# Eleven fixed homes for expert weights instead of nine and a one-time spare, sixteen experts written out, w1 and w3 split by contraction

## What is computed

```
for e in range(N_EXPERTS):                       # 16
    he = (silu(h @ w1[e]) * (h @ w3[e])) @ w2[e]  # w1, w3: 1024 x 512; w2: 512 x 1024
    out = out + combine[:, e:e + 1] * he          # 2 experts per token
```

## Time and profile before

| | us |
|---|---|
| median of 3 runs | 1133.92 (1132.99 to 1134.44) |
| the profiled execution | 1136.46 |
| its span, first to last instruction | 1134.6 |
| PE busy | 942.2 (83%) |
| DVE, ACT, POOL busy | 453.2, 248.2, 194.6 |
| HBM read | 306.72 MB |
| mean granted TensorE clock | 0.922 |

### The profile page before, as it was taken

How to read it: one execution, slowest core, us unless ns; L and a number is a source line. 1 busy time by engine, 2 the same in 40 slices (tenths; PEclk the granted TensorE clock), 3 DMA queues, 4 the chain that set the end, 5 groups by cost and what they waited for, 6 DMA issues and landing times.

```text
span 1134.6 us, 24010 instructions
## 1 busy us (share of the span) xinstructions
PE 942.2 (83%) x9000; PEld 550.9 (49%) x9001; DVE 453.2 (40%) x1074; ACT 248.2 (22%) x491; POOL 194.6 (17%) x328
## 2 busy tenths in 40 slices
PE   3999999988898499979888589999998477875795
PEld 2536446555445366645545266543654244442353
DVE  2178425555554423323222486416732422221223
ACT  2100112443322122313212131123521021210121
POOL 4100000110010144434323320001100111110011
PEclk9999999999989599999889789999998598997898
DMA  9997602830003989999999978317504989999991
GB/s 348 391 405 269 258 36 75 313 123 1 1 1 119 373 312 408 420 417 424 420 420 417 375 299 312 137 44 267 235 1 149 360 347 415 407 424 426 423 417 64
DMA packets 52335, 313.47 MB, mean 276 GB/s; under 512 B 6620, under 2 KB 7328, under 8 KB 33456
## 3 DMA queue, kind: packets, MB, share of 16 engines
q1 hardware_dynamic: 41168, 286.27, 62.7%
q0 software_dynamic: 8480, 18.05, 4.4%
q10 hardware_dynamic: 2624, 8.27, 2.0%
HBM read 306.72 MB, written 9.50 MB: 279 GB/s over the span
## 4 chain that ended last, share of the span: by engine, by line
PE 63%; DMA 23%; DVE 5%; issue 4%; DVEq 2%; SPq 1%; ACT 1%; POOL 0%; POOLq 0%; ACTq 0%
PE ps L1961 59%; DMA ring<-in_w 12%; DMA area<-in_w 5%; DMA HT<-in_w 3%; DMA ring<-in_w_in 2%; PE ps L2241 2%; DMA area<-h_rows,area 1%; PE ps L2070 1%; PE ps L2091 1%; DMA expert_rows<-area 1%; DVE area L1628 1%; DMA area<-expert_rows 0%; PE ps L2271 0%; PE ps L2260 0%; DVE area L1465 0%
## 5 line engine op out<-in xcount | busy, mean ns | idle before, releaser
L1961 PE MATMUL ps<-ring,area 128*32 128x256 f32 x3808 | 239.2, 399 | 48.8 <-DMA ring<-in_w 25.3
L1961 PE MATMUL ps<-area 128*32 128x256 f32 (+6 forms) x2328 | 245.6, 392 | 21.8 <-DVE area L1847 9.7
L1961 PE MATMUL ps<-ring,HT 128*128 128x512 f32 (+1 forms) x576 | 259.3, 604 | 2.1 <-ACT HT L1186 1.5
L1961 PEld LDWEIGHTS ps<-ring,area 128*32 128x32 f32 x3808 | 136.6, 115 | 140.3 <-issue 47.8
L1961 PEld LDWEIGHTS ps<-ring,HT 128*128 128x128 f32 x576 | 110.5, 197 | 128.7 <-issue 127.8
L1961 PEld LDWEIGHTS ps<-area 128*32 128x32 f32 (+3 forms) x2328 | 143.2, 144 | 57.3 <-issue 35.5
L1961 PE MATMUL ps<-HT,area 128*32 128x256 f32 x704 | 89.1, 409 | 37.4 <-DMA area<-in_w 20.8
L1875 DVE STREAM_TRANSPOSE area<-area 128x256 f32<-128x256 f32 x65 | 29.0, 446 | 199.8 <-PE ps L1961 197.0
L1961 PE MATMUL ps<-HT,ring 128*128 128x256 f32 (+1 forms) x320 | 88.1, 433 | 3.6 <-DMA ring<-in_w_in 3.4
L971 POOL DMA_INDIRECT area<-h_rows,area x68 | 70.9, 1043 | 102.8 <-DVEq L1860 42.3
L1961 PEld LDWEIGHTS ps<-HT,area 128*32 128x32 f32 x704 | 48.7, 118 | 72.5 <-issue 51.7
(11 more groups left out here) (229 smaller groups left out, 800.8 us busy)
## 6 DMA issues: line engine op xcount, KB each, us to landing
ring<-in_w SPq DMA_DIRECT2D x64, 2048.0 KB
ring<-in_w_ada SPq DMA_DIRECT2D x24, 2048.0 KB
area<-in_w SPq DMA_DIRECT2D x21, 1024.0 KB
ring<-in_w_in SPq DMA_DIRECT2D x10, 2048.0 KB
HT<-in_w SPq DMA_DIRECT2D x10, 2048.0 KB
area<-in_w SPq DMA_DIRECT2D x10, 2048.0 KB
ring<-in_w_out SPq DMA_DIRECT2D x4, 2048.0 KB
area<-expert_rows ACTq DMA_DIRECT2D x8, 512.0 KB, 7.2
```

The costliest lines, as they stand in the source:

```text
L1961: return t_.matmul(out, lhsT, rhs, start=first, stop=last_)
```

## The change

There are eleven homes in one turn through all 48 units. The spare place becomes a home like the others, and the eleventh ("late") is 12 KB per partition of new SBUF, gained by cutting the space for POOL's DMA descriptors from 16 to 4 KB per partition, and 4 KB of constants (`cst`, columns 128 to 1151: triangle, ones, rotation tables, masks) that the experts' stage doesn't read. Its first load waits for the slot choices (`oh_done`). Those constants are loaded again for layer 1, and ROWS1 moves out of `cst`. All loads and all sixteen experts are written out; waits are on constants. The first unit of an expert now holds the first half of the contraction for w1 and w3 together, the second the rest, so that TensorE waits for each at its own half. The order of the homes is HT, late, area, split, spare in layer 0 and HT, area, spare, late, split in layer 1. The blocks' arithmetic is the same.

```diff
-    w = w.reshape(DEPTH, E_N, 2, NG, KD, SLOT, 2, 2, SLOT, NCF)
-    w = w.transpose(0, 1, 6, 3, 5, 4, 7, 2, 9, 8)
+    w = w.reshape(DEPTH, E_N, 2, NG, 2, KD // 2, SLOT, NG, SLOT, NCF)
+    w = w.transpose(0, 1, 4, 3, 6, 5, 7, 2, 9, 8)
...
+        turn = [order[(len(names) + n) % RING] for n in range(RING)]
+        if l == 0:
+            turn += [HT_HOME, LATE_HOME, AREA_HOME, SPLIT_HOME, SPARE_HOME]
+        else:
+            turn += [HT_HOME, AREA_HOME, SPARE_HOME, LATE_HOME, SPLIT_HOME]
+        row, last = [], {}
+        for n in range(3 * E_N):
+            x = turn[n % HOMES]
+            row.append((x, uses[x]))
...
+            if x == LATE_HOME:
+                return [late[:], rows(cst[:, C_TRI:C_TRI + 2 * CHUNK])]
...
+                    if l and name == names[0]:
+                        x, u = max((y for y in EXPERTS[0] if y[0] == SPARE_HOME), key=lambda y: y[1])
+                        sp.wait_ge(ring_free[x], u + 1)
+                        for cnd in range(2):
+                            sp.dma_start(gate[:, cnd], modD[0, cnd:cnd + 1, 5 * D:6 * D].broadcast_to([P, D])).then_inc(gate2_in, 16)
+                        x, u = max((y for y in EXPERTS[0] if y[0] == LATE_HOME), key=lambda y: y[1])
+                        sp.wait_ge(ring_free[x], u + 1)
+                        sp.dma_start(cst[:, C_TRI:C_TRI + 2 * CHUNK], A["cst"][:, C_TRI:C_TRI + 2 * CHUNK]).then_inc(cst2_in, 16)
...
+                for n in range(3 * E_N):
+                    x, u = EXPERTS[l][n]
+                    first = n < HOMES
+                    if n >= RING:
+                        landed(sp, l, n - 2)
...
+                    if first and x == LATE_HOME:
+
+                        sp.wait_ge(oh_done[l], 1)
+                    if first and (x == SPLIT_HOME or x == AREA_HOME and l == 0):
+
+                        sp.wait_ge(pl_done, l + 1)
+                        sp.wait_ge(h2_out[l], 16 * (routed(l) // P))
+                        sp.wait_ge(gath[l][0], 16)
...
+                    if u:
+                        sp.wait_ge(ring_free[x], u)
...
+                dve.wait_ge(cst2_in, 32)
...
+                    pe.wait_ge(cst2_in, 32)
...
                     for k in range(KD):
                         lhsT = xT[:, k * SLOT:(k + 1) * SLOT]
+                        n, k_in = 3 * e + k // (KD // 2), k % (KD // 2)
+                        if arrive and k_in == 0:
+                            landed(pe, l, n)
...
-                expert(0, 0, 0, True)
-                for e in range(1, GROUPS + 1):
-                    expert(e, 0, e)
-                with pe.Fori(1, (E_N - 1) // GROUPS) as i:
-                    for q in range(GROUPS):
-                        expert(1 + q, i, 3 * i + 1 + q)
+                for e in range(E_N):
...
+                        if l == DEPTH - 1 or e < DRAINED:
+                            release = home(l, 3 * e - 1)
+                        elif e > DRAINED:
+                            free.append(home(l, 3 * e - 4))
...
-    nc = bacc.Bacc("TRN2", target_bir_lowering=False, num_devices=1)
+    nc = bacc.Bacc("TRN2", target_bir_lowering=False, num_devices=1, dynamic_dma_scratch_size=4096)
```

More of the change, by code:

```diff
@@ L43 @@
 RING = 6
-GROUPS = 3
-EXTRA = 3 * GROUPS - RING
+HT_HOME, AREA_HOME, SPLIT_HOME, SPARE_HOME, LATE_HOME = range(RING, RING + 5)
+HOMES = RING + 5
+DRAINED = 3
 LATE = (1, 1)
@@ L732, in ffn_rows @@
                 return X[:, 2:4]
-            rows = ring[:, EXPERTS[l][0][1][0]].rearrange("p k n -> p (k n)")
+            rows = ring[:, home(l, 3)].rearrange("p k n -> p (k n)")
             return rows[:, cnd * 2 * D:(cnd + 1) * 2 * D].rearrange("p (v d) -> p v d", v=2)
```

223 lines of the change are left out of this document (81 added, 142 removed).

## The result

The changed kernel took 1126.67 us, median of 7 runs (1122.18 to 1134.15), against 1134.44 us of the kernel before on the same chip; the ratio is 0.9934 [0.9908, 0.9961]. In a second series it was 1127.2 against 1134.21, again 0.9934 [0.9913, 0.9955]. So 7.5 us were won, where 17 were forecast.

The account below looks back on a forecast made before the run. It took DMA weight loading to bound the expert stages, with TensorE full elsewhere. 10.0 + 1.8 + 5.1 + 3.1 - 1.5 - 1.5 = 17.0 us saved, from a median of 1133.92 to 1117 us; range 1108 to 1127.

Parts of the forecast that it names:

- the second rival: Idle time only moved: cadence stretches or layer 0's end loses the gain; half the DMA gain goes, about 1125; 18 in 100.
- DMA idle time: Expert stages: earlier weight loads close holes in the DMA's work, winning 10.0 us in layer 0 and 5.1 in layer 1.
- (b): Sixteen experts written out: TensorE fetches code throughout and stalls at one jump on the tails; 1.5 us lost.
- The rival that I gave 6 in 100: Instruction fetch bounds the tails: 4.19 us at each of eight places, 1149 us in all; 6 in 100.
- Contraction halves: Expert stages' tails: half of one product starts on the first unit, winning 1.8 us in layer 0, 3.1 in layer 1.
- (a): End of layer 0: 0.5 MB of constants reloaded and output transfers meeting weights in flight; 1.5 us lost, bounds 0 and 3.5.
- Does the DMA still lead the last expert?: Last expert, both layers: yes; layer 0's unit 47 lands at 613.6, last product near 619; layer 1's 1105 and 1110.
- (c): Weight loads: more units in two pieces, their SP issues hidden and no cost in the DMA; 0 us.
- its rival of 6.6 us for nine: Units in pieces are slower: nine more such units at 0.73 us each, 1123.5 us in all; 8 in 100.
- (d): POOL: one DMA issue fewer and descriptor space cut to a quarter, with no wait for that space seen; 0 us.
- (e): SP issues: semaphore waits on constants in place of registers, under 0.4 us per issue, hidden; 0 us.

Follow-up runs that it names:

- b_unroll: Kernel before, with TensorE's loop of three experts replaced by experts written out, nothing else: 1144.23 us, ratio 1.0055.
- b_both: Kernel before, its nine homes kept, with TensorE's experts written out and w1, w3 in contraction halves: 1137.05 us, ratio 1.0021.
- both: Changed kernel, with nine steady homes and a loop of three for experts 7 to 15 in both layers: 1131.67 us, ratio 0.9982.
- b_halves: Kernel before, with w1 and w3 as contraction halves, the second half's wait behind the first half's products: 1133.19 us, ratio 0.9981.
- a_nocst: Changed kernel with ten homes (no late home), without the reload of constants ahead of layer 1 and its waits: 1128.73 us, ratio 0.9949.
- a_order: Changed kernel, with the late home's turn behind the first home that waits for the first gather, both layers: 1127.3 us, ratio 0.9926.
- a_latewait: Changed kernel, with the wait for w2 moved from ahead of the block loop into the product that uses it: 1124.74 us, ratio 0.9928.
- lw_again: Changed kernel with the wait for w2 moved into the product that uses it, measured a second time: 1125.91 us, ratio 0.9943.
- b_pieces: Kernel before, with its two extra homes' w1 and w3 units loaded as 12 KB and 4 KB a partition: 1136.69 us, ratio 1.0017.

## Why the prediction was half right

The measured 1126.7 lies inside the range of 1108 to 1127, at its very end. The direction was right, and the size was that of the second rival (about 1125, 18 in 100), not of the forecast. Of that rival's two mechanisms one is borne out, the loss at the end of layer 0; its time came out near by terms that it didn't have.

**DMA idle time, 10.0 and 5.1 us: right as a lead, wrong as a gain.** The late home was issued at 381.02 (near 382 forecast), the holes at 384 and 418 are gone, and at unit 17 the lead is 8.5 and 6.0 us. The step that failed is the one by which the expert stage "ends at: time at which the DMA starts, plus its idle time, plus its bytes, plus the tail". It takes the DMA for the bound of all that follows, with its cadence unchanged. Both halves of this fell. The cadence rose from 5.44 to 5.61 us in layer 0: 30 units of it are 5 us, and unit 47 went out at 609.5 where I had 603. That rise comes with the experts written out (5.54 us a unit from unit 27 on for 5.38, in b_unroll and b_both), and it leaves where they are a loop again (5.37, both); the DMA engines are busy in all of these, so late homes aren't its cause. And in layer 1 TensorE waited for no weights at all behind 900: 18.5 us more without a releaser, and 5.2 us more of busy time at a lower granted clock, stood in place of 26.2 us of waits for the DMA, so the DMA's lead couldn't shorten that stage by its length.

**(b), the written-out code, 1.5 us: mis-sized.** It costs 4.5 us beside the halves (b_both) and 6 alone (b_unroll), each give or take 4. I had found such stalls behind an expert of one block (2.63 and 1.56 us); they measure 1.8 to 7 us each, and, worse, I counted them on the tails alone, "so one jump". Nine of layer 1's sixteen experts have one block, and seven of the jumps behind them show such a wait. The other part of the cost I hadn't thought of: weights land more slowly beside written-out experts, in both layers (about 0.2 us a unit, table above). The rival that I gave 6 in 100 had the mechanism, on the same wrong places and with its price for all experts. The Trainium skill (Runtime: NRT & Kernel Launch, Instruction fetch mechanics) has prefetch mostly hidden and stalls at taken branches out of the window: the trace bears out the second half, 39.3 us of waits without a releaser against 20.8, and the first not everywhere: waits of 2.28, 3.95 and 3.20 us begin inside a product, in straight code. By how much layer 1 would be faster with eleven homes and no fetch wasn't tried: a loop of experts needs a turn of homes that comes round with it.

**Contraction halves, 1.8 and 3.1 us**: 2.2 us together by the ratio (b_halves), from nothing to 4.9 by the interval. Their mechanism is there in the stages, 2 and 5 us of one profile. By the ratio they are mis-sized by about half; whether they are, and where the rest went, isn't shown, since the stretch between was no longer in that profile (265.8 us).

**(a), the end of layer 0, 1.5 us: mis-sized.** I had named it, a fuller queue and 0.5 MB more, between 0 and 3.5. From the last expert product to the first transposes it is 3.6 us: 1.1 is the reload (a_nocst), and most of the rest goes with TensorE's last product standing nearer to the end of a queue that isn't shorter; the halves alone already cost 2.1 there. The read-back of the rows shares the engines with that queue's bytes and takes 7.3 us for 4.5. I had also misread the place: the scatter at 633.13 isn't the layer's last, two more follow it. Its counterpart after is the one at 628.49 (624.74 in the second profile), where I had 621. The rest of the 6 us between the layers is a step I hadn't priced at all: the late home's 2 MB stand ahead of each layer's first gather. The wait for the first tokens is 7.7 and 7.8 us in layer 1 for 5.2 and 4.7, and in layer 0 3.4 us hang on it (a_order). In the forecast the unit only filled a hole; the gather was in that hole.

**"Does the DMA still lead the last expert?"** I had unit 47 landed at 613.6. It landed at 620.5, behind an issue at 609.5, and the last expert's second block waited for it ahead of its loop, 1 to 2 us of that expert's 14.5 and 13.4; the time of the whole doesn't show them (a_latewait, lw_again).

**(c) pieces, 0**: for 20 more such units 2 us, at most 4 (b_pieces), so its rival of 6.6 us for nine is out. By the 341 GB/s that the Trainium skill (DMA: Bandwidth & Descriptors, Bandwidth) has for 1 MB, against 425 for 16 MB, my estimate was 0.76 us a unit; here it is 0.2 at most. **(d), (e)**: nothing in the profiles speaks against 0, and neither was tried alone.

By stages the forecast of -17 stands against: start +1.8 (0 forecast), layer 0's experts -8.6 (-11.8), between +6.1 (+1.5), layer 1's experts -3.4 (-8.2), tail -0.7 (0), with (b) (+1.5) within these. That is -4.9 by the profiles and -7.5 by the medians; where the other 2.6 us lie isn't shown.

What stays open: why beside written-out experts the DMA engines, busy all the while, moved fewer bytes a second. The window of b_unroll in layer 1 reads

```profile
950.00:1100.00 150.00, 109.14 (x1686) 62.23 (x1682) 30.80 (x91) 23.41 (x30) 18.23 (x30) 0.89 1.00 404
```

and that of before

```profile
950.00:1095.00 145.00, 105.56 (x1644) 59.10 (x1640) 30.07 (x88) 22.80 (x30) 18.16 (x30) 0.89 1.01 420
```

Some 13 more instruction packets, 0.2 MB, are too little for that by their bytes.

## What to carry to other kernels

Idle time of the bounding engine is worth its length only if whatever it waits on next moves too: before summing holes, ask for each later stretch whether that engine is still what is waited for, whether its cadence stays, and whether the lead has buffers in which to be kept. Count a cost that recurs per iteration (here a cold jump, one into code that has yet to be fetched) in every iteration, not only in the tail. And when a load is moved into a hole, ask what small urgent transfer was alone in that hole.

## What the runs showed of the hardware

- A cold jump costs more under load than I had thought: 1.8 to 7.3 us, at the same places in both profiles of the changed kernel, with the weights streaming beside it. One instruction packet of 16 KB took 1 us of an engine (0.8% of 16 engines over 225 us for 29 packets).
- Beside experts written out the same 2 MB units land further apart than beside a loop, at the same busy share: 5.54 for 5.38 us in layer 0 and 5.29 for 5.07 in layer 1 (b_unroll, before).
- Small transfers wait for what stands in the DMA engines, whichever queue they are in: the first gather 3.4 us behind 2 MB of weights, and the rows read back between the layers reach VectorE 12.1 us behind the last expert product for 8.5.
- Two executions of one program differed by 7.6 us with nearly the same waits (39.3 and 40.0 us without a releaser in layer 1): spans 1132.3 and 1124.7, at a mean granted clock of 0.924 and 0.929, with 3 us of it before the first expert product, 1 between the layers and 3 in layer 1's experts. A single profile of each kernel would have shown a gain of 2.3 us here.
